# A second transformer block worked by token tiles, with tile 1's top-64 selection placed behind tile 0's attention

## What is computed

```python
for i in range(4):
    h = rms_norm(x, norm_mix[i])
    kind = i % 3
    if kind == 0: y = dsa_mixer(h, ...)     # "selected": layers 0 and 3
    elif kind == 1: y = swa_mixer(h, ...)   # "window": layer 1
    else: y = mla_mixer(h, ...)             # "latent": layer 2
    x = x + y
    x = x + sqrelu_mlp(rms_norm(x, norm_mlp[i]), w_up[i], w_down[i])

def dsa_mixer(h, w_in, q_gain, k_gain, w_out, rel_bias):
    q, k, v, q_idx, k_idx, w_idx = split_cols(h @ w_in, [1024, 64, 64, 512, 64, 8])
    q, k = rms_norm(q, q_gain), rms_norm(k, k_gain)      # q by head of 64
    s_idx = einsum('bqhd,bsd->bqhs', q_idx, k_idx) * 64 ** -0.5
    score = einsum('bqh,bqhs->bqs', w_idx * 8 ** -0.5, relu(s_idx))
    score = where(admissible, score, -inf)
    _, sel = top_k(score, 64)                            # 64 keys of up to 256 for each token
    logits = q . k[sel] * 64 ** -0.5 + rel_bias[t5_bucket(rel)]
    return softmax(logits) . v[sel] @ w_out              # 16 heads
```

## Time and profile before

| | us |
|---|---|
| median of three runs | 3245.06 (3240.98 to 3248.14) |
| the profiled execution, and its span | 3243.43, 3241.6 |
| mixer 0 (with the bias layout), 1, 2, 3 | 212.7, 165.0, 167.3, 162.9 |
| an MLP | 179.8 |
| PE busy over the span | 2763.3 (85%) |
| mean granted clock of PE | 0.937 |

### The profile page before, as it was taken

How to read it: one execution, slowest core, us unless ns; L and a number is a source line. 1 busy time by engine, 2 the same in 40 slices (tenths; PEclk the granted TensorE clock), 3 DMA queues, 4 the chain that set the end, 5 groups by cost and what they waited for, 6 DMA issues and landing times. The chain is left out here.

```text
span 3241.6 us, 30642 instructions
## 1 busy us (share of the span) xinstructions
PE 2763.3 (85%) x10643; PEld 1689.3 (52%) x10643; DVE 1753.7 (54%) x3858; ACT 901.9 (28%) x1890; POOL 650.6 (20%) x628
## 2 busy tenths in 40 slices
PE   7887777777798877777777799999999889999999
PEld 3563222222346642222222365994689566975698
DVE  2447777777403377777775253553455374535454
ACT  1312222222104222222221122441344244423343
POOL 0014444444301144444444010000200000001000
PEclk9998999999997889999999887999699899999999
DMA  6229999999851089999999430643245133543253
GB/s 245 72 94 414 421 421 421 391 421 421 357 194 52 14 339 421 421 421 390 421 422 422 173 104 30 194 154 123 71 155 183 54 104 128 183 140 104 83 190 104
DMA packets 209649, 767.67 MB, mean 237 GB/s; under 512 B 16419, under 2 KB 87670, under 8 KB 143734
## 3 DMA queue, kind: packets, MB, share of 16 engines
q0 software_dynamic: 73728, 536.90, 40.0%
q1 hardware_dynamic: 135798, 229.25, 21.0%
HBM read 765.03 MB, written 1.07 MB: 236 GB/s over the span
## 5 line engine op out<-in xcount | busy, mean ns | idle before, releaser
L880 PE MATMUL psum<-weights,scratch 128*128 128x512 f32 x1224 | 586.5, 625 | 192.8 <-ACT scratch L1117 192.7
L755 PE MATMUL psum<-weights,xT 128*128 128x512 f32 (+2 forms) x1192 | 514.6, 594 | 10.7 <-ACT xT L1030 6.9
L880 PEld LDWEIGHTS psum<-weights,scratch 128*128 128x128 f32 x1224 | 229.7, 196 | 547.8 <-ACT scratch L1117 294.6
L880 PE MATMUL psum<-arena,scratch 128*128 128x512 f32 x824 | 395.0, 625 | 127.8 <-ACT scratch L1117 127.7
L1817 POOL DMA_INDIRECT weights<-in_peer_uv,scratch x306 | 345.4, 1129 | 483.0 <-PE psum L880 395.8
L1694 DVE TENSOR_TENSOR piece<-weights,piece 128x2048 fp32r<-128x2048 f32 x128 | 292.8, 2293 | 237.3 <-ACT piece L1159 237.3
L755 PEld LDWEIGHTS psum<-weights,xT 128*128 128x128 f32 x1192 | 231.5, 196 | 288.9 <-issue 273.6
L917 PEld LDWEIGHTS psum<-split_x,piece 128*128 128x128 f32 x3072 | 375.8, 192 | 7.2 <-DVE split_x L1702 2.4
L917 PE MATMUL psum<-split_x,piece 128*128 128x256 f32 x3072 | 378.3, 283 | 0.5 <-DVE split_x L1702 0.5
L934 PE MATMUL psum<-piece,hidden 128*128 128x512 f32 x1536 | 358.8, 390 | 0.0
L880 PEld LDWEIGHTS psum<-arena,scratch 128*128 128x128 f32 x824 | 154.9, 197 | 366.2 <-ACT scratch L1117 196.3
(11 more groups left out here) (195 smaller groups left out, 2485.3 us busy)
## 6 DMA issues: line engine op xcount, KB each, us to landing
weights<-in_w_up SPq DMA_DIRECT2D x64, 1024.0 KB, 5.5
weights<-in_w_down SPq DMA_DIRECT2D x64, 1024.0 KB, 5.0
weights<-in_w_qkv_a SPq DMA_DIRECT2D x6, 2048.0 KB, 20.0
weights<-in_a_w_in SPq DMA_DIRECT2D x6, 2048.0 KB, 15.5
weights<-in_peer_w_q SPq DMA_DIRECT2D x4, 2048.0 KB, 8.3
weights<-in_w_kv_b SPq DMA_DIRECT2D x4, 2048.0 KB, 13.1
weights<-in_a_w_out SPq DMA_DIRECT2D x4, 2048.0 KB, 7.8
weights<-in_b_w_in SPq DMA_DIRECT2D x3, 2048.0 KB, 11.0
```

The lines of the kernel that those rows point to most:

```text
L755: mm = pe.matmul(psum[g.bank][:, 0:w], xT[:, block0 + k, t * P:(t + 1) * P], c.view[:, k, c0:c0 + w], start=(k == 0), stop=(k == c.rows - 1))
L880: mm = pe.matmul(psum[g.bank][:, :], diagonal[:, j % DIAGONALS, :], row[:, D + half * BANK:D + (half + 1) * BANK], start=(j == pe_picks(t ...
```

## The change

In the second block each tile goes through a mixer as a program of its own, and the programs interleave on every engine.

- `TileProjection` plans column blocks for one tile at a time, and turns are planned by tile, on fewer banks. New counters `normed`, `prepared`, `heads_squared` and `down_done` say tile by tile what is ready. `Layer` has one plan for each kind (`plan_selected`, `plan_window`, `plan_latent`, then `plan_output`).
- PE, selected layer: tile 0's blocks, tile 1's last-but-one, tile 0's keys and index scores, further blocks of tile 1 with tile 0's queries and tile 1's keys between them, then `attend_tiles`: tile 0's attention, half of its output projection, tile 1's queries turned, the other half, tile 1's attention, its output projection with tile 0's turn for the MLP in it.
- DVE, selected layer: tile 0's queries, keys, index sum and selection, tile 1's keys and index sum, tile 0's attention, tile 1's queries and selection, tile 1's attention, which has the addition of tile 0's output to x in it. A tile's selection is a chain of its own.
- Two gains of queries are multiplied into the keys' (a product of both enters the score), whole for selected and window layers, for the latent layer the 64 unrotated columns. Its head squares go from DVE to ACT.
- All bridges of the second block are gone; only the first block's attention keeps its two.
- The masks of units have a ring of eight, in the place of the layer norms' gains. `split_x` moves to `y`.
- Sines and angles, the gains' turn and the bias rows are made at the program's start, the mirrored read is issued during the second expert layer, and the flips run behind its last matmul. ACT copies four flips, then gives the layer norm's root, then copies four.
- The last two pieces of an MLP's down projection are done for tile 0, then for tile 1 (`down_tile`), and DVE adds tile 0 to x and norms it in between (`mlp_to_x`). The MLP's first up piece waits for halves of its input. The output is stored by tile.

What it changes in order, at three places:

The diff, cut to its core:

```diff
-CLOCK_BRIDGE, CLOCK_BRIDGE_SELECT = (4, 9, 30), 16
-CLOCK_BRIDGE_START, CLOCK_BRIDGE_MLP = 2, 4
+CLOCK_BRIDGE_START = 2
+MASKS = 8
...
-        neg_logits, probs, probsT, masks3 = three(0), three(1), three(2), three(3)
+        neg_logits, probs, probsT = three(0), three(1), three(2)
+        relus8 = scratch[:, 0:IDX_HEADS * T].rearrange("p (b k) -> p b k", b=IDX_HEADS)
+        masks = ln_gb[:, :, :].rearrange("p a (b k) -> p (a b) k", k=T)
...
+        bias_groups = [group(4 + n % 4) for n in range(8)]
...
+            def plan_output(self, w_out, slots, turn0, turn1):
+                self.att.plan(0, HEADS)
+                self.out = TileProjection(column_chunks(w_out, D), slots, (6, 7))
+                out_turn0 = Turn(turn_tile(o, xT, 0), (4, 5))
+                out0 = self.out.plan(0, 0)
+                self.turn = [turn0, turn1()]
+                out0 += self.out.plan(0, 1)
+                self.att.plan(HEADS, NT * HEADS)
+                self.out_turn = [out_turn0, Turn(turn_tile(o, xT, 1), (4, 5))]
+                out1 = self.out.plan(1, 0)
+                mlp0 = Turn(turn_tile(o, xT, 0), (0, 1))
+                out1 += self.out.plan(1, 1)
+                self.out_blocks = [out0, out1]
+                self.mlp_turn = [mlp0, Turn(turn_tile(o, xT, 1), (2, 3))]
...
+            scored = peer1.s[1][3]
+            sp.wait_ge(psum_freed[scored.bank], scored.freed)
...
             sp.wait_ge(bias_written, 16)
             mirrored = bass.AP(bias_rows.tensor, 0, [[1, P], [384, HEADS], [1, T]])
-            sp.dma_start(bias_mirrored, mirrored).then_inc(bias_read, 16)
+            sp.dma_start(bias_mirrored, mirrored).then_inc(mirrored_loaded, 16)
...
+                            if n == 0 and b == 0 and k % 4 == 0:
+                                pe.wait_ge(x_low.sem, m.x_low0 + 3 + k // 4)
...
-                keep_clock(m.up[0], CLOCK_BRIDGE_MLP)
-                pe.wait_ge(x_low.sem, m.x_low0 + 4)
...
+                n, q = PIECES // 2 - 2, PIECES - 2
+                down_ready(n, q)
+                down_tile(n, q, 0)
+                down_ready(n + 1, q + 1)
+                down_tile(n + 1, q + 1, 0).then_inc(down_done.sem, 1)
+                down_tile(n, q, 1).then_inc(piece_used.sem, 1)
+                down_tile(n + 1, q + 1, 1).then_inc(piece_used.sem, 1)
...
+            def selected(l):
+                project(l.in0[0], turned=l.x_turn[0])
+                turn_normed(l.x_turn[1], l.normed0 + 1)
+                for n in range(1, 4):
+                    project(l.in0[n])
+                project(l.in1[2], turned=l.x_turn[1])
+                turn_prepared(l.key_turn[0], l.k_ready[0])
+                index_scores(l.index[0])
+                project(l.in1[3])
+                pe.wait_ge(prepared.sem, l.q_ready[0] + 1)
+                turns(l.turn[0])
+                project(l.in1[0])
+                turn_prepared(l.key_turn[1], l.k_ready[1])
+                index_scores(l.index[1])
+                project(l.in1[1])
+                copied(l.turn[0].last)
...
+            def attend_tiles(l):
+                kind = KINDS[l.kind]
+                attend(l.att, kind, 0, HEADS)
+                copied(l.att.v[HEADS // l.att.per - 1])
+                turns(l.out_turn[0])
+                project(l.out_blocks[0][0:1], turned=l.out_turn[0])
+                pe.wait_ge(prepared.sem, l.q_ready[1] + 1)
+                turns(l.turn[1])
+                project(l.out_blocks[0][1:2])
+                copied(l.turn[1].last)
+                attend(l.att, kind, HEADS, NT * HEADS)
+                copied(l.att.v[-1])
+                turns(l.out_turn[1])
+                project(l.out_blocks[1][0:1], turned=l.out_turn[1])
+                turn_normed(l.mlp_turn[0], l.normed0 + 2)
+                project(l.out_blocks[1][1:2])
+                turn_normed(l.mlp_turn[1], l.normed0 + 3)
...
-                keep_clock(l.turn.groups[0][2], CLOCK_BRIDGE[l.kind])
-                pe.wait_ge(in_ready.sem, l.q_ready + 1)
-                turns(l.turn)
-                copied(l.turn.last)
+                turn_normed(l.x_turn[0], l.normed0)
                 if l.kind == 0:
-                    index_scores(l.index)
-                    keep_clock(l.att.v[1], CLOCK_BRIDGE_SELECT)
...
+                root(l.root["k1"], 1)
+                turns(l.key_turn[1])
+                relus(l.index[1])
+                outputs(l.in1[1], to_y)
+                exps(l.att, None, 0, HEADS)
+                root(l.root["q1"], HEADS)
+                turns(l.out_turn[0])
+                turns(l.turn[1])
...
+            def mlp_to_x(l, t):
+                m = l.mlp
+                if t == 0:
+                    dve.wait_ge(down_done.sem, m.down0 + 1)
+                else:
+                    dve.wait_ge(piece_used.sem, m.used0 + PIECES)
+                for half, g in enumerate(m.down[t]):
+                    part = x[:, t, half * BANK:(half + 1) * BANK]
+                    dve.tensor_tensor(part, part, psum[g.bank][:, :], ALU.add).then_inc(psum_freed[g.bank], 1)
 
...
+            def input_tiles(l, before):
+                normed_input(l, 0, "n0")
+                turns_with_gain(l.x_turn[0], l.n * KB)
+                if before:
+                    mlp_to_x(before, 1)
+                normed_input(l, 1, "n1")
+                turns_with_gain(l.x_turn[1], l.n * KB)
+            def selected(l):
+                queries(l, 0, prepared.sem)
+                selected_keys(l, 0)
+                index_sum(l.index[0])
+                select(0)
+                selected_keys(l, 1)
+                index_sum(l.index[1])
+                attend(l.att, "selected", l.mask0, None, 0, HEADS)
+                queries(l, 1, prepared.sem)
+                select(1)
...
+            def attended(l):
+                mask0, sink0 = None if l.kind == 2 else l.mask0, l.sink0 if l.kind == 1 else None
+                attend(l.att, KINDS[l.kind], mask0, sink0, HEADS, NT * HEADS, lambda: add_to_x(l.out_blocks[0], 1.0))
+                normed_input(l, 2, "m0")
                 low_part(l.mlp, 0)
                 low_part(l.mlp, 1)
-                for t in range(NT):
-                    add_to_x(l.out, 1.0, t)
-                    normed_input(l.mlp_squares, l.mlp_root, t)
-                turns_with_gain(l.mlp_turn, 4 * KB + l.n * KB, KB)
-                split_input(l)
+                turns_with_gain(l.mlp_turn[0], 4 * KB + l.n * KB)
+                split_input(l, 0)
+                add_to_x(l.out_blocks[1], 1.0)
+                normed_input(l, 3, "m1")
+                turns_with_gain(l.mlp_turn[1], 4 * KB + l.n * KB)
+                split_input(l, 1)
...
-            def unit_masks(l):
-                for u in range(NT * HEADS):
-                    h, t, nk = unit(u)
-                    if u >= 3:
-                        pool.wait_ge(psum_freed[l.att.s[u - 3].bank], l.att.s[u - 3].freed)
+            def unit_masks(l, t, before):
+                for u in range(t * HEADS, (t + 1) * HEADS):
+                    h, _, nk = unit(u)
+                    user = l.att.s[u - MASKS] if u >= MASKS else before.att.s[u - MASKS] if before else None
+                    if user:
+                        pool.wait_ge(psum_freed[user.bank], user.freed)
                     other = sel_mask[:, t, 0:nk] if l.kind == 0 else const_at("window_mask")[:, T - nk:T]
-                    pool.tensor_tensor(masks3[:, u % 3, 0:nk], bias8[:, h, T - nk:T], other, ALU.add).then_inc(mask_ready.sem, 1)
+                    pool.tensor_tensor(masks[:, u % MASKS, 0:nk], bias8[:, h, T - nk:T], other, ALU.add).then_inc(mask_ready.sem, 1)
+            pool.wait_ge(psum_freed[bias_row_group.bank], bias_row_group.freed)
+            pool.dma_start(bias_rows, scratch[0:HEADS, 0:384]).then_inc(bias_written, 16)
```

835 lines of the change are left out of this document (496 added, 339 removed).

## The result

The changed kernel takes 3190.73 us (median of four runs, 3188.67 to 3191.59), the kernel before 3244.88 in the same comparison: a ratio of 0.983, interval 0.982 to 0.985. It is 1.7% faster, by a third of what was forecast (3088, range 3057 to 3148), and lies above the range. The profiled execution took 3188.67 us with a span of 3187.0, 54.6 less than the span before. PE's mean granted clock fell from 0.937 to 0.928.

A forecast was written before the change was run, and what follows sets the result against it. PE sets the pace, with worthless busy time and lost clock as reserves. 3243.4 + 0.7 - 45.0 - 44.1 - 46.5 - 25.2 - 18.3 - 2.2 = 3062.8; plus 18.4, 5 and 1.6 gives 3088 us, range 3057 to 3148.

The forecast's parts named there:

- Attention: Second block's attentions: units run at the latent layer's 0.58 and 1.10 us; tile 0 12.6, tile 1 21.5, together 34.1.
- The ring: Masked attentions: summed-mask buffers growing from 3 to 8 mean POOL no longer holds the scores back.
- Attentions fall to half clock: Rival, second block's attentions: two tile-1 ones cold give 3133, all eight 3234; two likeliest; chance 0.27.
- Cold starts: Second block after idle PE: eight starts at half clock, two of them MLPs, 2.3 us each, 18.4 in all.
- Block 1: First block: moved by a handful of instructions (sine tables, a bias row, a POOL DMA), +0.7 us.
- The front: Block 1's end to layer 0's first projection: bias DMA hidden, flips earlier, tile 0 alone normed; -18.3 us.
- the wait for the root of key 1: Layer 0 before attention: root stands behind tile 1's first query block's eviction on ACT, 2.3 us.
- tile 1's selection: Selected layers, DVE: about 9.2 us, covered by tile 0's output projection on PE with some 4.7 us margin.
- Between the tiles: Tile 0's attention to tile 1's: 14.9 us of PE work and 3.6 of hand-over and root wait ahead.
- The latent layer: Layer 2: DVE bounds its first half; 120.8 us against 167.3 before, -46.5.
- hand-overs: Between queues, those the profile rows do not show: 5 us added to the sum.
- The weighed rule: Latent layer's attention: skill page says transposes do not engage full clock; prediction followed the trace row, a warm start.

The follow-up runs named there:

- e5: e1 with the ring of summed masks cut from eight buffers to four: 3122.11 us, 0.962 of the kernel before.
- e1: Changed kernel with two groups of bridge matmuls put back into the filling of each second-block attention: 3126.62 us, 0.964 of the kernel before.
- e10: Changed kernel, no second-block bridges, selected and window scores contracting 128 rows (two heads summed): 3109.61 us, 0.955 of the kernel before.
- e3: Changed kernel with the mirrored bias read issued behind the second expert layer's last value matmul: 3192.73 us, 0.984 of the kernel before.
- e7: e1 with more bridges where second-block work started cold (behind attentions, ahead of output projection, MLP, key turn): 3099.30 us, 0.956 of the kernel before.
- e4: Changed kernel with tile 1's selection moved back ahead of tile 0's attention on DVE: 3187.13 us, 0.982 of the kernel before, runs spread over 38 us.
- e12: Kernel before with six bridge groups instead of two at each attention's start, block 1's differential attention included: 3263.17 us, 1.004 of the kernel before.
- e11: Kernel before with selected and window scores contracting 128 rows (two heads summed): 3170.62 us, 0.974 of the kernel before.
- e14: e7 with keys laid out twice, zero-padded to 128 rows, and without the bridge groups filling attentions: 3089.64 us, 0.952 of the kernel before.

## Why the prediction was wrong

**Attention.** The step that failed: "the units should run as the latent layer's, which needs no masks". It held two errors. The ring was taken for what paced a masked unit, and e5 and layer 3 of the kernel before refute it: the pace is PE's, 0.85 and 1.39 us with 64-row scores, whether the ring has three, four or eight buffers. That is 17.3 us. And with the ring gone the units were held to be dense enough to keep the clock, an argument made from latent units, which put 96 rows to work, and with the filling at their start taken away. That is 61.5 us, and e1 and e10 show that either the filling or 128-row scores bring most of it back. Layer 3 of before, at 1.00 with 64-row scores, was read as the rule with layers 0 and 1 as the accident; in the changed kernel none of the six held.

**The rival.** "Attentions fall to half clock" named the event. Its prices a piece, 22.6 and 13.9, were too high (over the sum's 21.5 and 12.6 the six are 15.8 and 10.5 dearer), its count of two too low, and it was given 0.27. Its own evidence, two of three masked attentions cold in the profile before, should have made it the likeliest case. That evidence was also misread: layer 0 fell within some 6 us of its first unit, but layer 1 kept 1.00 for 14 us, through all its tile-0 units, and fell in tile 1, with PE busy and the ring of three in place.

**Cold starts.** 2.3 us each was about right (2.4 for layer 0's first output block, 9.39 against 7.03; 1.2 to 2.9 for an MLP; the prediction's 2.7 from six blocks is 2.4, since six at 27.73 / 4 are 41.6 and not 41.2), but all four MLPs started cold, 9.3 in all, not two.

**Block 1.** "Moved by a handful of instructions" was wrong: +15.7. The read was priced at nothing since PE did not wait for it; the cover was a phase with no bandwidth to give. e3 shows 10.5 of it, and 4.7 lies ahead of the stick-breaking attention.

**The front** was right in its own stretch (17.6 of 18.3), but with the read in block 1's account some 7 us of it are earned.

**Right to within a microsecond:** layer 0 from its first projection to attention (61.5, predicted 61.3), the wait for the root of key 1 (2.32, predicted 2.3), tile 1's selection (9.1, predicted 9.2) and its cover, the end, and under 2 us from an MLP to the next projection. Between the tiles of layer 0 18.5 was predicted; it is 21.6 with a cold block and 18.4 in e7. The latent layer is 4.2 off, and that is partly luck: its tile-0 attention was at 1.00 in the profiled run, while in e3 and e4, with the same instructions there, it fell to 0.62 and the layer took 130.3 and 130.7 us, not 125.0. With e7's clock the four stages are 6.3, 8.6, 4.2 and 4.5 above their sums, 23.6 in all: the 17.3 of the units, and 6.3 more, near the 5 that was put in for hand-overs.

**The weighed rule.** The prediction went by the earlier trace rows that transposes alone bring the clock up, and the changed kernel shows it again, in the turn ahead of the latent layer's attention and then two windows of a microsecond from it:

```profile
2564.31 6.14 PE L851 MATMUL psum<-const,y 128*96 128x128 f32 x32 [3.85 <-DVE y L1584]
```

```profile
2569.00:2570.00 1.00, 1.00 (x10) 0.98 (x9) 0.97 (x2) 0.82 (x2) 0.00 (x0) 0.82 1.14 373
2570.00:2571.00 1.00, 0.45 (x5) 0.19 (x2) 0.97 (x2) 1.00 (x3) 0.00 (x0) 1.00 1.03 343
```

The attention behind them starts at 1.00 and stays there in this run. The Trainium skill, page "TensorE: Matmul & The Clock Gate", section "Part 4: PE-mode transpose", says the full clock does not engage for transposes; these rows contradict it for turns done as matmuls by a constant.

## What to carry to other kernels

Take the price of a unit from a stage with the same shapes at full clock: the 0.85 and 1.39 stood in layer 3 of the kernel before. Before a stage is called dense enough to hold TensorE's clock, compare its matmuls with those of a stage that held it, by rows of the array and by columns too, and if they differ price the stage cold as well. Where operands have half the rows, zeros in the other half may be cheaper than the half clock and the longer unit. A transfer moved off the path is free only where the DMA engines have room: price it by what runs beside it.

## What the hardware showed that was not expected

- A PE busy in 64.80 of 64.80 us had a granted clock of 0.58 (e12); with 128 rows in the scores, and busy for 29.47 of 30.10, it had 1.00 (e11).
- Block 1's differential attention, with the same 64-row scores and values of 128 columns instead of 64, had 1.00 over 38.90 us, busy for 38.61.
- Score matmuls on 64 rows between matmuls on 128 cost 0.28 to 0.29 us a unit at full clock against scores on 128 rows.
- Attentions with the same instructions can differ: in e1 tile 0 held at 1.00 in layer 0 and fell to 0.65 in layer 3. The latent tile 0 held at 1.00 in the changed kernel and fell to 0.61 or 0.62 in e3, e4, e10 and e14.
- The same 2 MB took 8.0 us behind the gathers and 46.4 beside gathers at 421 GB/s, and the stretch with them grew from 818.8 to 829.2 us.

## What stays open

Whether it is the number of rows at work, the alternation of 64 and 128 rows, or that of the two halves of the array from head to head that lets the clock go: every experiment changed all three. Why the differential attention, which has all three, keeps its clock. Why layer 3 of the kernel before kept its clock with the instructions of layer 0. And of block 1's 15.7 the 4.7 ahead of the stick-breaking attention, which no run took apart and which vary by more than that among kernels that do not differ there.
